# Projections and down halves of a two-layer fp32r kernel: products of 256 columns in place of 512

## What is computed

```python
# first block
z = rms_norm(x) @ w_in                      # then an HGRN2 scan and a band attention
merged = gate_a * (y_a @ w_branch_a) + gate_b * (y_b @ w_branch_b)
h = x + merged @ w_out                      # "out" projection, 2048 x 2048
u = rms_norm(h)
h = h + square(relu(u @ w_up)) @ w_down     # w_up 2048 x 8192, w_down 8192 x 2048
h = rms_norm(h)
# second block
proj = rmsnorm(concat([meta, h])) @ w_in_2  # then two attentions, gates
y = concat([ya, yb]) @ w_out_2              # "out2" projection, 2048 x 2048
out = h + rmsnorm(y)
```

## Time and profile before

| | |
|---|---|
| median of 3 runs | 1892.37 us (1891.93 to 1894.53) |
| the profiled execution | 1891.33 us |
| its span | 1889.5 us |
| granted TensorE clock | 0.999 of full |
| TensorE busy | 1874.0 us, 99% of the span |
| VectorE, ScalarE, GpSimd busy | 1101.6, 889.1, 149.8 us |

### The profile page before, as it was taken

One profiled execution on the slowest core, in us unless ns is written; L12 is line 12 of the kernel. 1 busy time (PEld: TensorE's weight loads), 2 busy tenths in 40 slices (PEclk: granted clock), 3 DMA queues, 4 the chain that ended last, 5 costly groups with the idle time before them and its releaser, 6 DMA issues.

```text
span 1889.5 us, 33863 instructions
## 1 busy us (share of the span) xinstructions
PE 1874.0 (99%) x13420; PEld 1739.9 (92%) x13420; DVE 1101.6 (58%) x1270; ACT 889.1 (47%) x1171; POOL 149.8 (8%) x133
## 2 busy tenths in 40 slices
PE   9999999999999999999999999999999999999998
PEld 9989998999999889988998899899889999899986
DVE  6655766567655555555445544554565556767664
ACT  6534444455544445443444344344454345674543
POOL 1001322411001100000010000001010000000000
PEclk9999999999999999999999999999999999999999
DMA  8656555566565656656665665566556665354454
GB/s 274 192 179 172 183 179 177 166 198 182 166 232 191 215 183 179 196 197 192 196 192 193 193 193 192 193 194 190 189 180 179 178 180 155 111 164 146 156 191 143
DMA packets 176915, 347.75 MB, mean 184 GB/s; under 512 B 11152, under 2 KB 11360, under 8 KB 176256
## 3 DMA queue, kind: packets, MB, share of 16 engines
q1 hardware_dynamic: 174176, 337.76, 57.2%
q0 software_dynamic: 2608, 8.08, 1.7%
HBM read 342.37 MB, written 2.10 MB: 182 GB/s over the span
## 4 chain that ended last, share of the span: by engine, by line
PE 96%; DVE 2%; ACT 1%; issue 0%; DMA 0%; SPq 0%; DVEq 0%; ACTq 0%
PE ps L445 58%; PE ps L457 33%; PE ps L547 1%; DVE wlo L1288 1%; PE ps L770 1%; PE ps L737 1%; PE ps L760 1%; ACT whi L886 0%; PE ps L780 0%; DMA raw<-in_w_in_dram 0%; PE ps L475 0%; PE ps L748 0%; PE ps L598 0%; PE ps L590 0%; DVE xlo L1310 0%
## 5 line engine op out<-in xcount | busy, mean ns | idle before, releaser
L1288 DVE TENSOR_TENSOR wlo<-raw,whi 128x1024 fp32r<-128x1024 f32 x631 | 796.7, 1269 | 694.2 <-ACT whi L886 693.2
L886 ACT ACTIVATE whi<-raw 128x1024 fp32r<-128x1024 f32 x631 | 664.3, 1058 | 882.7 <-PE ps L445 552.5
L445 PE MATMUL ps<-xhi,whi 128*128 128x256 f32 (+1 forms) x1904 | 541.5, 284 | 0.2 <-DVE wlo L1288 0.2
L445 PE MATMUL ps<-xhi,wlo 128*128 128x256 f32 (+1 forms) x1904 | 530.9, 279 | 0.0
L445 PE MATMUL ps<-xlo,whi 128*128 128x256 f32 x1664 | 462.1, 278 | 0.0
L445 PEld LDWEIGHTS ps<-xhi,whi 128*128 128x128 f32 x1904 | 359.2, 189 | 8.4 <-issue 6.5
L445 PEld LDWEIGHTS ps<-xhi,wlo 128*128 128x128 f32 x1904 | 357.8, 188 | 0.0
L445 PEld LDWEIGHTS ps<-xlo,whi 128*128 128x128 f32 x1664 | 313.0, 188 | 1.3 <-issue 0.5
L445 PE MATMUL ps<-x2hi,whi 128*128 128x256 f32 x1024 | 282.8, 276 | 0.0
L445 PE MATMUL ps<-x2lo,whi 128*128 128x256 f32 x1024 | 282.7, 276 | 0.0
L445 PE MATMUL ps<-x2hi,wlo 128*128 128x256 f32 x1024 | 282.7, 276 | 0.0
(11 more groups left out here) (371 smaller groups left out, 2368.5 us busy)
## 6 DMA issues: line engine op xcount, KB each, us to landing
raw<-in_w_in_dram SPq DMA_DIRECT2D x279, 512.0 KB, 3.8
raw<-in_w_up_dram SPq DMA_DIRECT2D x128, 512.0 KB, 3.7
raw<-in_w_down_dram SPq DMA_DIRECT2D x128, 512.0 KB, 3.6
raw<-in_w_out_dram SPq DMA_DIRECT2D x64, 512.0 KB, 4.0
raw<-in_w_branch_a_dram SPq DMA_DIRECT2D x16, 512.0 KB, 4.7
raw<-in_w_branch_b_dram SPq DMA_DIRECT2D x16, 512.0 KB, 4.0
x_nat<-in_x_dram SPq DMA_DIRECT2D x4, 512.0 KB, 7.0
rel<-in_rel_turned_dram POOLq DMA_DIRECT2D x8, 256.0 KB, 4.3
```

What stands on the lines that cost most here:

```text
L445: ins = mm(outs[b], w[:, k % SLOTS, j, cols], v, start=start, stop=last and j == CK - 1 and i == 2, skip_group_check=True)
L886: f(whi[:, k % SLOTS], raw[:, k % SLOTS], ACT.Copy).then_inc(whi_ready, 1)
L1288: tt(wlo[:, k % SLOTS], raw[:, k % SLOTS], whi[:, k % SLOTS], ALU.subtract).then_inc(wlo_ready, 1)
```

## The change

`chunk_n` gets an argument `pieces`. With pieces = 2 each 512-column product becomes two of 256 columns that write the two halves of the same PSUM bank: first the three parts for columns 0 to 255, then the three for columns 256 to 511. So the chunk has 24 products, and each activation piece is loaded into the array twice as often. `start` (which marks the bank as fresh) is kept for the first product of piece 0 alone. With pieces = 1 the chunk is as before.

The callers choose: `w_out` and the down halves use two pieces, but one piece in chunk k = 2 behind the transposes, and in the last chunk (k = 7) of the last group. `w_out_2` uses two pieces, but one in its very first chunk. The four column groups of `w_in` stay at one piece.

```diff
-            def chunk_n(c0, k, kt0, xh, xl, s, first, last, halves=range(NT)):
+            def chunk_n(c0, k, kt0, xh, xl, s, first, last, halves=range(NT), pieces=1):
                 pe.wait_ge(wlo_ready, c0 + k + 1)
                 for j in range(CK):
                     kt = kt0 + j
                     for t in halves:
                         toks = slice(t * P, (t + 1) * P)
-                        for i, (v, w) in enumerate(((xh, whi), (xh, wlo), (xl, whi))):
-                            ins = mm(ps[:, 2 * s + t, :], v[:, kt, toks], w[:, k % SLOTS, j, :],
-                                     start=first and j == 0 and i == 0,
-                                     stop=last and j == CK - 1 and i == 2, skip_group_check=True)
+                        for piece in range(pieces):
+                            cols = slice(piece * CW // pieces, (piece + 1) * CW // pieces)
+                            for i, (v, w) in enumerate(((xh, whi), (xh, wlo), (xl, whi))):
+                                ins = mm(ps[:, 2 * s + t, cols], v[:, kt, toks], w[:, k % SLOTS, j, cols],
+                                         start=first and j == 0 and i == 0 and piece == 0,
+                                         stop=last and j == CK - 1 and i == 2, skip_group_check=True)
...
-                    chunk_n(C_OUT + NC * n, k, CK * k, uhi, ulo, n % 2, k == 0, k == NC - 1)
+                    whole = n >= 1 and k == 2 or n == 3 and k == NC - 1
+                    chunk_n(C_OUT + NC * n, k, CK * k, uhi, ulo, n % 2, k == 0, k == NC - 1, pieces=1 if whole else 2)
...
-                        chunk_n(c0 + 4 * NC + NC * g, k, CK * (k % (NC // 2)), uh, ul, g % 2, k == 0, k == NC - 1)
+                        whole = last and g >= 1 and k == 2 or g == 3 and k == NC - 1
+                        chunk_n(c0 + 4 * NC + NC * g, k, CK * (k % (NC // 2)), uh, ul, g % 2, k == 0, k == NC - 1,
+                                pieces=1 if whole else 2)
...
                 return chunk_n(C_OUT2 + NC * g, k, CK * (k % (NC // 2)), yt_hi[mixer], yt_lo[mixer],
-                               out2_set(g), k == 0, k == NC - 1, halves)
+                               out2_set(g), k == 0, k == NC - 1, halves, pieces=1 if g == 0 and k == 0 else 2)
```

## The result

The changed kernel takes 1897.74 us (median of 6 runs, 1896.76 to 1898.13), the kernel before 1891.76 us beside it (1890.81 to 1894.53). The ratio is 1.0026, 95% interval 1.0016 to 1.0036: slower by some 0.3%, where 0.24% faster was forecast. The time lies above the range. It is the rival that I had given 0.13, "the slow pace is caught", but larger than I had sized it, and for the most part in places that I had not looked at.

What follows compares the result with a forecast made beforehand. TensorE's product pace was taken as the bound; -4.79 us for 180 cut chunks and +0.18 us for seven returns gave -4.61 us, a median of 1887.8 us, range 1886.0 to 1893.5.

Steps and rivals of the forecast that it cites:

- the slow pace is caught: Returns to 256 columns behind whole chunks: 67 chunks run at 117.9 ns, +2.5 us, 1894.9 us; chance 0.13.
- the operand rival: Cut chunks: the surcharge belongs to streaming weights, not width; 114.4 ns a product, only 0.18 us stays, 1892.5; chance 0.13.
- the other bound: Cut chunks at the second pace of 117.9 ns: 2829 ns a chunk, 82 more than before.
- The rival of a fixed price for each product: Cut chunks: every weight-streaming product pays 15.6 ns above its columns, 187 ns a chunk, 33.7 us, 1926; chance 0.04.
- the way back at 900.69: Return from 512 to 256 columns, five distances in 0.59 us: 25 ns each for seven whole chunks, 0.18 us more.
- the 87.08 us: Down halves: window expected in the profile after, 31 cut chunks and one whole, in place of 87.90 us.
- The estimate by the Trainium skill's page: Cut chunks: columns / 2.4 plus a fixed 2.5 ns per product, 30 ns a chunk, 5.4 us slower.
- Both have fast precedents: New streams, entered from a fast 256-column stream or a 512-column chunk, were both taken to run at 113.3 ns.
- What stands ahead of the transposes is now a 256-column product ... and I cost it at nothing: Six places ahead of transposes: the 256-column product there costs nothing, within 10 ns each.
- the six precedents: All six places in the trace where 256-column products directly follow a 512-column chunk; all settle in the fast pace.
- The precedent for the transposes: The up half's chunk ahead of 731.10, already a 256-column product ahead of transposes; used to cost that order at nothing.
- a pace is kept until something else comes through: TensorE's pace as a lasting state of the pipe: 113.3 or 117.9 ns for 256-column products.

Runs made afterwards that it cites:

- the first experiment: Against the kernel before, only the down halves of quarters 0 to 2 cut into 256-column products (93 chunks): 1892.07 us against 1893.3, ratio 0.9994.

## Why the prediction was wrong

**Right: the bound, and the two prices.** TensorE's pace set the time. No wait of TensorE was added, no evacuation came late. A cut chunk in the fast pace costs 2720 ns as taken from the up halves (87.07 us a half), so streaming weights makes no difference and the operand rival is out. In the slow pace it costs the 82 ns more that were given as the other bound. The rival of a fixed price for each product is out as well: a fast cut chunk is cheaper than a whole one. Two slips in the working weigh nothing: 12 x 228.9 is 2746.8 ns and not 2746.6, and the way back at 900.69 is 23 ns and not 25; the 87.08 us is 87.07 by its own sum.

The estimate by the Trainium skill's page "TensorE: Matmul & The Clock Gate", section "Back-to-back issue gap" (1897.8), is near the time that was measured, but by coincidence: by it each of the 180 chunks would be dearer by 30 ns, and none is (120 are 26.6 ns cheaper, 60 are 82 ns dearer). The section gives this formula for a single product by itself; for a stream of weight loads and products it has some 131 ns for 512 columns. The trace disagrees with both: 228.9 ns.

**Wrong: the choice between the two paces.** The step that failed is "Both have fast precedents", with "What stands ahead of the transposes is now a 256-column product ... and I cost it at nothing". Two faults lie in it.

First, the six precedents were not of the kind that the change makes. They were returns from 72 or 384 products of 512 columns into `chunk_t`; the change makes returns from 12, behind transposes, which are themselves behind a 256-column product. The two-whole-chunk run shows that 24 do no better than 12, the run with nothing whole behind the transposes that the stream is slow there even with no return at all, and the run with a whole chunk ahead of the transposes that what stands ahead of them matters: where a 256-column product stood ahead of the transposes, 36 of 39 returns were slow; where a 512-column one did, four of eight, and those behind group 2 were fast all four times. The precedent for the transposes, the up half's own behind a 256-column product, is the very place that turned slow. The trace of before held the warning: most of the slow stretches of the earlier trace rows's kind begin behind transposes and other small products.

Second, I had written that a pace is kept until something else comes through, and yet priced it in the cut chunks alone. It is carried from one code into the next: from the up half into the down half, and in the run with `w_out` alone even into 384 products of 512 columns. It does end: behind the 744 slow products of quarter 0's down half stands one whole chunk, and the up half behind that (line 445) is fast again:

```profile
908.19:995.25 87.06, 87.06 (x768) 87.03 (x767) 1.00 0.64 192
```

TensorE around the up half's eight transposes, first in the kernel before, then in the changed one:

```profile
729.51 0.28 PE L445 MATMUL ps<-x2hi,wlo 128*128 128x256 f32 x1
...
730.19 0.28 PE L445 MATMUL ps<-x2hi,wlo 128*128 128x256 f32 x1
730.30 1.04 PE L475 MATMUL ps<-ident,h 128*128 128x128 f32 x8
...
731.99 0.28 PE L445 MATMUL ps<-x2lo,whi 128*128 128x256 f32 x1
```

```profile
731.56 0.28 PE L445 MATMUL ps<-x2lo,whi 128*128 128x256 f32 x1
...
732.01 0.28 PE L445 MATMUL ps<-x2hi,wlo 128*128 128x256 f32 x1
732.13 1.04 PE L477 MATMUL ps<-ident,h 128*128 128x128 f32 x8
732.92 0.36 PE L445 MATMUL ps<-x2hi,whi 128*128 128x256 f32 x1
733.12 0.28 PE L445 MATMUL ps<-x2lo,whi 128*128 128x256 f32 x1
...
733.59 0.28 PE L445 MATMUL ps<-x2hi,wlo 128*128 128x256 f32 x1
```

Ahead of the transposes both run at the fast pace (six distances in 0.68 us, four in 0.45), the transposes are the same, and behind them one settles at 113.3 (six distances in 0.69 us from 731.30 to 731.99, the first of them 120 ns) and the other at 118 (four in 0.47). So the visible pace does not hold the whole state: something finer, the phase, is carried through a 512-column chunk, 48 fast products and eight transposes. The run with a whole chunk ahead of the transposes says so too. From the whole chunk behind group 3's transposes up to the last quarter its code is that of the changed kernel, the 96 products behind that are as slow (11.31 us in both traces) and the 48 of the up half as fast (5.46 us), and yet its up half was fast and that of the changed kernel slow.

The slow pace made 3.2 us in the unedited up half and then 3.3 us (2.5 lost and 0.8 not gained) in the down half. The rival in the prediction had 67 chunks behind whole ones, +2.5 us. Of those 29 were slow (18 in `w_out`, 11 in the last quarter) and 38 fast; it had neither of the two larger pieces.

**What is not settled.** Shown is that the loss lies in stretches at the slow pace and not in the cut chunks as such: the two kernels that avoid the bad entries have none of it (124 and 140 chunks cut), and four dummy transposes gave 5.6 us back with every chunk still cut. Shown is also that in `w_out` and quarter 0 the pace follows from the order of TensorE's instructions: it came again in the repeated trace and in every kernel with that order. What the phase is, is open, and so is a rule for it.

Two places warn against one. The first is group 1's return in the last quarter. From quarter 1 on five kernels (six traces) have the same code up to its transposes, and 240 products at 113.3 ns stand ahead of them in each. It was fast in both traces of the changed kernel and with two whole chunks, and slow in the three kernels with dummies some 600 us earlier. The 168 products in the changed kernel and in the one with four dummies (line 459):

```profile
1374.37:1393.41 19.04, 19.04 (x169) 19.00 (x167) 1.00 0.58 186
```

```profile
1367.82:1387.61 19.79, 19.79 (x169) 19.74 (x167) 1.00 0.62 186
```

Whether that is carried over 600 us or is chance, no run tells.

The second is in the kernel before. It already has the helper `shift_phase`, three transposes (line 505, called on lines 649, 655 and 812). Its call in `w_in`, near 380 us, stands between 72 slow products and 144 more. The changed kernel there, in its first trace and in its second:

```profile
380.10 0.49 PE L510 MATMUL ps<-ident,acc 128*128 128x128 f32 x3
380.34 0.37 PE L445 MATMUL ps<-xhi,whi 128*128 128x256 f32 x1
380.55 0.28 PE L445 MATMUL ps<-xlo,whi 128*128 128x256 f32 x1
...
381.12 0.28 PE L445 MATMUL ps<-xhi,whi 128*128 128x256 f32 x1
```

```profile
379.62 0.49 PE L510 MATMUL ps<-ident,acc 128*128 128x128 f32 x3
...
380.06 0.28 PE L445 MATMUL ps<-xlo,whi 128*128 128x256 f32 x1
...
380.54 0.28 PE L445 MATMUL ps<-xhi,wlo 128*128 128x256 f32 x1
```

Five distances in 0.57 us, 114 ns, against four in 0.48, 120: the same instructions of the same kernel, fast once and slow once. Over all fifteen traces the slow pace ended there in eleven. So three transposes can end it, and that three failed and four worked at the one place in quarter 0 gives no number to rely on. The three came from that helper and wrote three column ranges, and the four wrote one range four times; a second place was tried with four alone.

## What to carry to other kernels

When the bound is a stream of products on one engine, measure distances between starts stretch by stretch, and look for two values in identical code before costing an edit: the edit may be worth less than the choice between them. A change that touches TensorE's order anywhere can move the cost of unedited stretches behind it (with `w_out` alone cut, up to 180 us behind its end), so compare the traces stretch by stretch and not only where the diff is. Here the form that held was to cut products only in long streams that are entered fast, and to leave 512-column products on both sides of the transposes: 124 or 140 chunks for 0.2%, where 180 chunks gave a loss.

## What the runs showed of the hardware that was not expected

TensorE streams fp32r products of 128 x 128 weights at two stable paces with the clock granted in full: 113.3 or 117.9 ns for 256 columns, 228.9 or 233.3 ns for 512. (The slow one of 512 columns stands in five traces: in the run with `w_out` alone cut, and in the four in which the stretch near 62 us below was slow, in the 120 products of `w_in` behind it.) A pace lasts through long streams: the slow one held for 1463 distances in a row in the changed kernel (719 in the up half and 744 in the down half of quarter 0). Within the streams of 72 products or more it changed at a wait near 21 us alone; elsewhere only where another shape stood between, and not always then.

The two paces also account for differences between traces where nothing was edited. Near 30 us stands a stretch of 264 products and near 62 us one of 360, the same instructions in all fifteen traces. The first was slow in ten of them and the second in four, and `w_out` began between 633.9 and 637.3 us; at 4.6 ns a product the two are worth 1.2 and 1.7 us. There it does fall by chance, as it does near 380 us, while the returns of `w_out` were slow 21 times out of 21. That a good part of the scatter of the runs (1890.6 to 1895.7 us for the kernel before, over the runs beside all experiments) comes from this is likely, but single runs have no trace, so it was not shown; it would also be why the ratio of the first experiment tells less than its trace.
